# Sums of squares as one-column products, the second norm's factor moved to h, x1 made in chunks: one decoder layer on one core

## The reference

```python
xn = rmsnorm(x, norm_mix_pre)
x  = x + rmsnorm(W_o(sum_b sigmoid(g_b(xn)) * P_b(mixer_b(xn))), norm_mix_post)
hn = rmsnorm(x, norm_ffn_pre)
h  = hn @ w_up                        # 2 * 5632 columns: a gate half and a value half
hc = conv_b + sum(conv_w[i] * he[:, i:i + T] for i in range(3))   # he: two rows of history, then h
f  = (gelu(gate half of hc) * value half of hc) @ w_down
y  = x + rmsnorm(f, norm_ffn_post)

def rmsnorm(x, g):
    y = x * rsqrt(mean(x * x, -1) + 1e-6)
    return y * g
```

## Time and profile before

| | |
|---|---|
| median of 3 runs | 2102.45 us (2101.04 to 2105.14) |
| profiled execution | 2102.59 us, of this 2100.8 from the first to the last instruction (the span) |
| granted TensorE clock, mean of the span | 0.974 of full speed |
| instructions | 37670 |
| HBM | 374.87 MB read, 47.09 MB written |

### The profile page before, as it was taken

The page is one execution under the profiler, slowest core; times in us unless marked ns, Lnnn a source line. Parts: engine busy times, 40 slices in busy tenths (PEclk is TensorE's granted clock), DMA queues, the critical chain, the costliest instruction groups (busy, mean ns, idle before and its releaser), DMA issues.

```text
span 2100.8 us, 37670 instructions
## 1 busy us (share of the span) xinstructions
PE 2000.3 (95%) x15905; PEld 1918.4 (91%) x15905; DVE 1066.8 (51%) x1065; ACT 754.7 (36%) x641; POOL 94.5 (4%) x180
## 2 busy tenths in 40 slices
PE   7999996799999999999999699999999999999995
PEld 5999994599999999999999599999999999999994
DVE  4333334453444443445753656565665565565564
ACT  4333332334333433333333234333333333333332
POOL 0000002000000000000000101000000000000001
PEclk9999997799999999999999899999999999999998
DMA  6454522376666776766675234556566556566532
GB/s 240 162 173 163 185 80 80 125 253 213 220 223 226 253 254 209 227 198 233 245 233 170 80 121 161 163 177 216 200 211 222 195 204 223 203 212 205 204 119 61
DMA packets 187432, 396.15 MB, mean 189 GB/s; under 512 B 10745, under 2 KB 19985, under 8 KB 185786
## 3 DMA queue, kind: packets, MB, share of 16 engines
q1 hardware_dynamic: 182236, 359.38, 52.1%
q10 hardware_dynamic: 4567, 32.23, 3.8%
q0 software_dynamic: 528, 3.08, 0.5%
HBM read 374.87 MB, written 47.09 MB: 201 GB/s over the span
## 4 chain that ended last, share of the span: by engine, by line
PE 93%; DVE 5%; ACT 1%; issue 0%; DMA 0%; ACTq 0%; SPq 0%; DVEq 0%
PE ps L1556 27%; PE ps L1558 27%; PE ps L1557 27%; PE ps L1538 3%; PE ps L1544 1%; DVE m_T L1090 1%; PE ps L1812 1%; PE ps L1769 1%; PE ps L1775 1%; DVE w_lo L1073 1%; PE ps L1707 0%; PE ps L1800 0%; DVE stat L1083 0%; DMA x_nat<-in_x_prompt 0%; DVE vn L1178 0%
## 5 line engine op out<-in xcount | busy, mean ns | idle before, releaser
L1556 PE MATMUL ps<-xn_hi,w_hi 128*128 128x288 f32 x3104 | 922.0, 297 | 16.9 <-DVE xn_lo L1096 13.8
L1558 PE MATMUL ps<-xn_hi,w_lo 128*128 128x288 f32 x3104 | 917.5, 296 | 0.0
L1557 PE MATMUL ps<-xn_lo,w_hi 128*128 128x288 f32 x3104 | 916.0, 295 | 0.0
L1073 DVE TENSOR_TENSOR w_lo<-w_raw,w_hi 128x2048 fp32r<-128x2048 f32 (+1 forms) x272 | 614.4, 2259 | 570.7 <-ACT w_hi L727 570.7
L727 ACT ACTIVATE w_hi<-w_raw 128x2048 fp32r<-128x2048 f32 (+1 forms) x272 | 514.1, 1890 | 1018.8 <-PE ps L1558 1006.1
L1556 PEld LDWEIGHTS ps<-xn_hi,w_hi 128*128 128x128 f32 x3104 | 584.6, 188 | 25.6 <-DVE xn_lo L1096 15.4
L1557 PEld LDWEIGHTS ps<-xn_lo,w_hi 128*128 128x128 f32 x3104 | 584.6, 188 | 0.0
L1558 PEld LDWEIGHTS ps<-xn_hi,w_lo 128*128 128x128 f32 x3104 | 584.3, 188 | 0.0
L1556 PE MATMUL ps<-act_hi,w_hi 128*128 128x288 f32 x704 | 207.9, 295 | 2.8 <-DVE act_lo L1457 2.8
L1558 PE MATMUL ps<-act_hi,w_lo 128*128 128x288 f32 x704 | 208.5, 296 | 0.0
L1557 PE MATMUL ps<-act_lo,w_hi 128*128 128x288 f32 x704 | 207.9, 295 | 0.0
(11 more groups left out here) (266 smaller groups left out, 1529.6 us busy)
## 6 DMA issues: line engine op xcount, KB each, us to landing
w_raw<-in_w_in SPq DMA_DIRECT2D x104, 1024.0 KB, 6.6
w_raw<-in_w_up SPq DMA_DIRECT2D x88, 1024.0 KB, 5.0
w_raw<-in_w_down SPq DMA_DIRECT2D x44, 1024.0 KB, 5.2
k_half<-in_cache_k SPq DMA_DIRECT2D x64, 256.0 KB, 3.4
v_half<-in_cache_v SPq DMA_DIRECT2D x64, 256.0 KB, 3.3
w_raw<-in_w_o SPq DMA_DIRECT2D x16, 1024.0 KB, 5.2
out<-in_cache_win ACTq DMA_DIRECT2D x32, 512.0 KB, 4.4
w<-in_cache_win SPq DMA_DIRECT2D x40, 256.0 KB, 4.4
```

Of the source, the lines that this page charges most:

```text
L1073: e.tensor_tensor(w_lo[s][:, 0:k, 0:n], w_raw[slot][:, 0:k, 0:n], w_hi[s][:, 0:k, 0:n].bitcast(F32), ALU.subtract).then_inc(lo_ready, 1)
L1556: e.matmul(dst, w_hi[s][:, r, cols], x_hi[:, k0 + r, :], start=first and r == 0, stop=False)
L1557: e.matmul(dst, w_hi[s][:, r, cols], x_lo[:, k0 + r, :], start=False, stop=False)
L1558: mm = e.matmul(dst, w_lo[s][:, r, cols], x_hi[:, k0 + r, :], start=False, stop=last and r == k - 1)
```

## The change

Four things change.

- **Sums of squares.** The squares are first added together on DVE (`add_squares`), and PE then multiplies 128 tokens of squares as the stationary matrix with one column of ones (`col_sums`), so that the sums lie with tokens on the partitions: 128x3. Variance, root and reciprocal run on these three columns. A diagonal matrix with the factor and one product with ones bring it back to every partition.
- **The second norm's factor** is no longer applied to x1. `xn_hi` and `xn_lo` hold x1 times the gain alone, and `h_out` multiplies h by the factor as it takes it out of PSUM. For that `h_out` moves from ACT to DVE.
- **x1 in chunks.** `residual` makes x1 in eight chunks of 1, 1, 2, 2, 2, 2, 2 and 4 rows of 128; ACT and DVE make `xn_hi` and `xn_lo` chunk by chunk, and PE starts round 0 with the first.
- **Smaller moves.** W_o's groups get their gain at the copy from PSUM; the `hist_c` copy goes from DVE to ACT; `m_T` is cleared by POOL; at the end the squares stand ahead of the copies of `tail_rows`, and the factor is read from PSUM.

The core of the diff:

```diff
+        def x1_squares(q):
+            if q >= 2:
+                e.wait_ge(dve.sem, dve.at(("ffn_pre", "sum", q - 1)))
+            s = 1 if q == 1 else 0
+            e.activation(sq_x[s][:, :, :], x1[:, 4 * q:4 * q + 4, :], ACT.Square)\
+                .then_inc(act.sem, act.step(("ffn_pre", "sq", q)))
...
-        root("mix_post")
+        out_squares(3)
+        hi(ffn_unit(0, 1))
+        col_root("mix_post")
+        e.wait_ge(pe.sem, pe.at("histc"))
+        e.activation(view(hist_c, P, 0, [[1, 1408]]), view(ps, P, 0, [[1, 1408]]), ACT.Copy)\
+            .then_inc(act.sem, act.step("hist_c"))
+        high_chunks(0, 8)
+        hi(ffn_unit(0, 2))
+        high_chunks(8, 12)
+        hi(ffn_unit(0, 3))
+        high_chunks(12, 16)
         for q in range(4):
...
+            x1_squares(q)
...
-            h_out(i, 0, u0 + 4)
             hi(ffn_unit(i, 6))
...
-            h_out(i, 1, u0 + 8)
             e.wait_ge(conv_step, i * 24 + 12)
...
+        residual(0, 1)
+        residual(1, 1)
+        low_chunks(0, 1)
+        residual(2, 2)
+        low_chunks(1, 4)
+        lo(ffn_unit(0, 1))
+        residual(4, 2)
+        residual(6, 2)
+        low_chunks(4, 8)
+        lo(ffn_unit(0, 2))
...
+        def h_out(i, s, done):
+
+            e.wait_ge(unit_done, done)
+            e.wait_ge(conv_step, i * 24)
+            e.wait_ge(tails_put, i * 6)
+            e.wait_ge(pool.sem, pool.at(("H0", 1)))
+            e.wait_ge(act.sem, act.at(("ffn_pre", "rstd")))
+            e.tensor_tensor(H[s][:, :, 2:HS], ps[:, 4 * s:4 * s + 4, 0:NP_TOK],
+                            view(stat, P, 2 * TOK, [[0, 4], [1, NP_TOK]]), ALU.mult).then_inc(h_copied, 1)
...
+            h_out(i, 0, u0 + 4)
             conv_pair(i, 0, 0)
-            lo(ffn_unit(i, 7))
+            if down:
+                lo(ffn_unit(i, 7))
             conv_pair(i, 0, 2)
...
                 lo(ffn_unit(i, 9))
                 y_add(i, 0, ffn_unit(i, 8))
                 lo(ffn_unit(i, 10))
+            h_out(i, 1, u0 + 8)
             conv_pair(i, 1, 0)
...
+        def col_sums(tag, bank, at, sq, first):
+            for c in range(4):
+                for m, t0 in enumerate((0, P, TOK - P)):
+                    mm = e.matmul(ps[:, bank, at + m:at + m + 1], sq[:, c, t0:t0 + P], ones[:, 0:1],
+                                  start=first and c + m == 0, stop=False, skip_group_check=True)
+            return mm
...
+                    if fixed and i == 0 and s == 1 and j == 0:
+                        e.wait_ge(dve.sem, dve.at(("ffn_pre", "sum", 3)))
+                        col_sums("ffn_pre", 2, 288, sq_x[1], True).then_inc(pe.sem, pe.step(("ffn_pre", "ss")))
```

More of the change, by code:

```diff
@@ L687, in _ @@
         e.wait_ge(landed["x_back"], 16)
[L688 to L694, removed]
+        e.wait_ge(dve.sem, dve.at(("x1", 12)))
+        for q in range(4):
+            e.memset(m_T[:, 4 * q:4 * q + 4, :], 0.0).then_inc(y_added, 1)
+        e.wait_ge(act.sem, act.at("hist_c"))
         for s in range(2):
@@ L964, in _ @@
                 g = n // 4 - 1
[L965 to L968, removed]
-        root("mix_post")
-        for q in range(4):
[L971 to L987, removed]
+                out_squares(g)
+                for c in range(4):
+                    k = NORM["mix_post"] + 4 * g + c
+                    e.activation(m_T[:, 4 * g + c, :], ps[:, 4 * (g % 2) + c, 0:TOK], ACT.Identity,
+                                 scale=gains[:, k:k + 1]).then_inc(m_copied, 1)
+        out_squares(3)
[9 more added lines that the diff above has]
+        high_chunks(12, 16)
+        for q in range(4):
+            x1_squares(q)
         def act_high(i):
@@ L1017, in ffn_round @@
             window_copy(i, 0)
-            if early:
+            if early and down:
                 hi(ffn_unit(i, 2))
@@ L1021, in ffn_round @@
                 act_high(i)
-            for j in range(3 if early else 2, 6):
+            for j in range((3 if down else 4) if early else 2, 6):
                 hi(ffn_unit(i, j))
@@ L1025, in ffn_round @@
                     window_copy(i, j // 2)
-            h_out(i, 0, u0 + 4)
             hi(ffn_unit(i, 6))
+            if not down:
+                col_root("ffn_pre")
             hi(ffn_unit(i, 7))
+            if not down:
+                e.wait_ge(pe.sem, pe.at(("ffn_pre", "rstd")))
+                e.activation(view(stat, P, 2 * TOK, [[144, 2], [1, 144]]), view(ps, P, 288, [[512, 2], [1, 144]]), ACT.Copy)\
+                    .then_inc(act.sem, act.step(("ffn_pre", "rstd")))
             window_copy(i, 3)
@@ L1049, in _ @@
         hi(ffn_unit(11, 3))
+        e.wait_ge(tails_put, 66)
+        for q in range(4):
+            squares("ffn_post", m_T, sq_f, q, [(y_added, 4 + 4 * 10 + q + 1)])
         e.wait_ge(lo_ready, 272)
@@ L1055, in _ @@
             .then_inc(act.sem, act.step("tail_rows"))
-        for q in range(4):
-            squares("ffn_post", m_T, sq_f, q, [(y_added, 4 + 4 * 10 + q + 1)])
-        root("ffn_post")
+        col_root("ffn_post")
         for m in range(3):
@@ L1411, in _ @@
[L1411 to L1420, removed]
@@ L1421, in _, with add_squares, col_variance @@
-        variance("ffn_pre", 3, D_MODEL, ("ffn_pre", "ss", 3))
-        rstd("ffn_pre")
-        norm("ffn_pre", xw_b, x1, lambda q: None)
+        def add_squares(tag, sq, into, what, ready):
+            for q in ready:
+                e.wait_ge(act.sem, act.at((tag, "sq", q)))
+            e.tensor_tensor(into, sq, into, ALU.add).then_inc(dve.sem, dve.step((tag, "sum", what)))
+        def col_variance(tag, bank, at):
+            e.wait_ge(pe.sem, pe.at((tag, "ss")))
+            e.tensor_scalar(col[:, 0:3], ps[:, bank, at:at + 3], 1.0 / D_MODEL, EPS, ALU.mult, ALU.add)\
+                .then_inc(dve.sem, dve.step((tag, "var")))
@@ new lines, in low_chunks @@
+        def low_chunks(c0, c1):
+            for c in range(c0, c1):
+                g = NORM["ffn_pre"] + c
+                e.wait_ge(act.sem, act.at(("ffn_pre", "hi", c)))
+                e.scalar_tensor_tensor(out=xn_lo[:, c, :], in0=x1[:, c, :], scalar=gains[:, g:g + 1],
+                                       in1=xn_hi[:, c, :].bitcast(F32), op0=ALU.mult, op1=ALU.subtract)\
+                    .then_inc(dve.sem, dve.step(("ffn_pre", "lo", c)))
+        for j in range(2, 17):
+            lo(unit_no(U_GATE, 8, 0, j))
+            if j == 11:
+                add_squares("mix_post", sq_b[:, 0], sq_b[:, 1], 1, (0, 1))
+                e.wait_ge(dve.sem, dve.at(("mix_post", "sum", 1)))
+            if j == 15:
+                add_squares("mix_post", sq_b[:, 1], sq_b[:, 2], 2, (2,))
@@ L1474, in ffn_round @@
                 lo(ffn_unit(i, 1))
-            if fixed:
+            if fixed and down:
                 lo(ffn_unit(i, 2))
@@ L1482, in ffn_round @@
                 act_low(i)
-            for j in range(3, 7):
+            u0 = ffn_unit(i, 0)[0]
+            for j in range(3 if down else 4, 7):
                 lo(ffn_unit(i, j))
+            if not down:
+                col_variance("ffn_pre", 2, 288)
+                col_rstd("ffn_pre")
+                lo(ffn_unit(i, 7))
+            h_out(i, 0, u0 + 4)
             conv_pair(i, 0, 0)
-            lo(ffn_unit(i, 7))
+            if down:
+                lo(ffn_unit(i, 7))
             conv_pair(i, 0, 2)
@@ L1546, in sums, with unit @@
             mm.then_inc(pe.sem, pe.step((tag, "ss", q)))
-        def unit(no, x_hi, x_lo, k0, side, first, last, k=SEG, n=4):
+        def col_sums(tag, bank, at, sq, first):
+            for c in range(4):
+                for m, t0 in enumerate((0, P, TOK - P)):
+                    mm = e.matmul(ps[:, bank, at + m:at + m + 1], sq[:, c, t0:t0 + P], ones[:, 0:1],
+                                  start=first and c + m == 0, stop=False, skip_group_check=True)
+            return mm
+        def unit(no, x_hi, x_lo, k0, side, first, last, k=SEG, n=4, fresh=False):
             u, _, _, s = no
@@ L1948, in _ @@
                     unit(unit_no(U_GATE, 8, i, 4 * g + j), M_hi, M_lo, 4 * j, g, j == 0, j == 3)
-        e.wait_ge(m_copied, 3)
-        for q in range(4):
-            sums("mix_post", sq_b, q, 3)
+        e.wait_ge(m_copied, 12)
         e.wait_ge(landed["crow"], 16 * 8)
```

127 lines of the change are left out of this document (98 added, 29 removed).

## The result

The change is slower: 2169.26 us (median of 4 runs, 2165.68 to 2170.57) against 2102.91, a ratio of 1.0313 with a 95% interval of 1.0295 to 1.0332. The profiled execution took 2170.57, its span is 2168.8, the mean granted clock 0.957.

What follows compares the result with a forecast made beforehand. PE, busy 95%, was taken to bound the kernel, so any wait inside a round adds in full. 2102.6 + 74.7 (ten rounds) - 10 - 8 (the two ends) gave 2159 us, range 2138 to 2172.

Steps and rivals of the forecast that it cites:

- The mechanism: Rounds 1 to 10: unit 9 waits 5.83 us for h_out(i,1) on DVE, behind y_add(i,0) and w_lo of unit 10.
- Case B: Ahead of unit 9: h_out(i,1) is through before unit 8 ends, so no wait; 2084.6 us, chance 0.05.
- The clock's term: Behind unit 9's wait, 17 products at the 1.2 GHz level lose 1.64 us per round, bounds 0 and 1.64.
- Case A: Rounds 1 to 10: the stalls come without a clock loss; 2143 us, chance 0.08.
- The sum: Whole kernel: 2102.6 plus 74.7 for the rounds, less 10 and 8 for the two ends, 2159.3 us.
- part 2: From the last W_o unit to the first FFN products: 27.6 us earlier, mostly given back; 10 gained, 6 to 16.
- part 3: End of the kernel: sums, scaling and adds finish sooner, 8 us gained, bounds 5 to 10.
- main case: Whole kernel: waits ahead of unit 9 less gains at both ends, 2159 us, ends 2135 and 2171, chance 0.83.
- Case C: Feed-forward rounds: POOL's copies of the tails hold DVE's convolution, 11 us more, 2171; chance 0.04.

Runs made afterwards that it cites:

- The early version: The change with h_out(i,1) on DVE moved between w_lo of unit 8 and w_lo of unit 9, ahead of y_add(i,0): 2089.89 us.
- The third experiment: The change plus 14 extra fp32 products on PE, results thrown away, between y_add(i,0) and unit 9 of each of ten rounds: 2148.04 us.
- the second experiment: The change with h_out(i,1) moved between y_add(i,0) and w_lo of unit 10: 2128.32 us.
- the last experiment: The early version, with ACT copying the last norm's factor from PSUM to SBUF for the 16 scalings: 2092.03 us.

## Why the prediction was right, point by point

**The mechanism** held to the row: the place (unit 9 of rounds 1 to 10), the releaser (`H` by DVE) and the order behind unit 8's end. A wait of 5.83 was forecast and an idle time of 5.73 came; `h_out` took the 1.42 that it had been given (1573.38 to 1574.80). Case B ended the other way for the reason given: neither `y_add(i,0)` nor w_lo of unit 10 can start before unit 8 ends. The early version is what case B described, and at 2089.89 it lies near the 2084.6 worked out for it.

**The clock's term** was right in kind and too small: 1.64 per round were taken and called the upper bound too, "since a longer wait costs no second restart". A round takes 84.40 us ((2080.76 - 1321.20) / 9, the first and the last of the ten waits), 8.1 over 76.3. The third experiment, in which the clock did not fall, puts 6.0 of this down to the wait and 2.1 to the clock. The 2.1 is a mean: behind the ten waits between 11 and 25 products came at 0.24 us, a loss of 1.4 to 2.8. Behind 1574.92 and behind 1827.68 it is, over 4 us:

```profile
1575.00:1579.00 4.00, 4.00 (x21) 0.65 0.72 255
1828.00:1832.00 4.00, 4.00 (x18) 0.50 0.68 249
```

So the 1.64 of the earlier trace rows was no ceiling. It was no floor either: behind the 2.85 of the second experiment nothing was lost in four rounds of ten, and in the third experiment the wait of the earlier trace rows itself, again 2.81, was followed by a clock of 1.00 (2085 to 2089). Nor is a wait just above the 1.55 of the earlier trace rows safe: after one of 1.96, at 998.37 in the kernel before, the clock was 0.50 from 1000 to 1002. A single row was taken for a fixed price; the price varies from wait to wait, and what decides it stays open.

Ten rounds came to 81.2 for 74.7, which is 6.5 of the 10 us by which 2159 was too low, about 1.6 of them wait and 4.9 clock. Case A, no clock loss, would have been 2143; the experiment with extra products brought it about and came to 2148.

**The sum.** In the profiled execution 11.3 us lie between 2159.3 and 2170.6: 6.5 from the rounds, 2.6 from part 2, 2.5 from the spread ahead of W_o's end, less 0.3 from part 3. The upper end of the main case, 2171, had been built from a dearer `h_out` and smaller gains. A dearer `h_out` did not come; that the clock's excess fitted into the same room is luck.

**Part 2** gave 7.4 where 10 were taken and 6 to 16 allowed. The first product came 13.5 us after W_o's end (1173.75 to 1187.23), not 11.75. Of these 1.7 us the one-column products are 1.5: 7.06 for 5.6. The waits ahead of units 2 to 4 were smaller than forecast (1.47, 1.90 and 4.06 for 1.8, 2.0 and 6.1), and there was none ahead of unit 1. The clock went the other way: two restarts, 3.2 us, were counted, but behind the start of units 3, 4 and 5 the products lost about 5.6 us at the 1.2 GHz level, after waits of 1.90 and 4.06 and, in unit 5, after the one-column products of the second norm. Two of these stretches:

```profile
1212.00:1216.00 4.00, 3.67 (x16) 0.57 0.20 79
1236.00:1240.00 4.00, 4.00 (x21) 0.57 0.25 50
```

That part 2 came out near its forecast is in part two errors that cancelled: 3.5 us less of waits, about 2.4 more of clock.

**Part 3** gave 8.3 for 8. The split between its steps was not foreseen: the one-column products took 8.45 for 5.6 to 6.6, and scaling from 2146.60 came 13.9 after the last `y_add` began, where it was 18.6 before, so 4.7 earlier and not 7. The scalings and adds made up for it. What scaling and adds themselves gave is 3.1 (from the first scaling's start to the last add's end 14.45 before, 11.32 now): the scalings were no longer held beside POOL's add, but DVE's own adds were, 2.18 for 1.36.

The rule that the prediction cited from the Trainium skill, "SBUF — State Buffer", section "SBUF: two separate sides" (a VectorE operation with two SBUF inputs and a GpSimd operation that reads SBUF exclude each other for a whole instruction), agrees with the trace of the last experiment: eight scalings take 5.88 with the factor in SBUF and 3.49 with it in PSUM.

**Case C** didn't come: the first tap beside POOL's copy took 0.86 for 0.78, and the second and third taps, which read two SBUF tensors, took 528 ns on average in both kernels. But the earlier trace rows had been read wrongly. The copy ran 1.14 there and ended as w_lo ended, and now it takes:

```profile
1574.96 0.19 POOL L705 COPY tails<-H 128x8 f32 x1 [24.51 <-DVE H L1507]
```

All 22 of these copies took 1.12 to 1.14 us before, and 0.19 to 0.36 now. So by these rows it was POOL that waited for DVE in the kernel before; the row said nothing of what POOL would do to DVE.

## What to carry to other kernels

In all rows shown here DVE took its operations in the order written, waiting at each until it could start. So an operation that frees a buffer must not stand behind one that needs the work which waits for that buffer. When a step moves to another engine, list what stands ahead of it there and what each of those waits for: engine shares (DVE was at 51%) say nothing about it, and here a shift by three places in the order is worth 81 us.

A wait of PE inside a dense stretch can cost more than its length, and not the same each time: nothing or 1.5 us more behind waits of 2.85, 1.4 to 2.8 more behind waits of 5.73. Take the price from several waits at least as long, or leave both ends open.

Where a small gain has to be seen under a larger spread, cut both spans at the same events and compare stretches; medians gave 3.5 us for an end that is worth 8.

## What the runs showed of the hardware that was not expected

The clock also fell while PE was busy without a pause. During the 48 records of one-column products behind W_o the granted clock went from 1.00 to 0.50, and the records came half as often:

```profile
1175.00:1177.00 2.00, 2.00 (x22) 1.00 0.67 260
1177.00:1179.00 2.00, 2.00 (x18) 0.86 0.00 0
1179.00:1181.00 2.00, 2.00 (x11) 0.50 0.00 0
```

PE shows no idle time in these stretches; what it did ahead of the fall were these products. In the kernel before, the sums over 288 columns stand at this place, and from 1171 to 1179 the granted clock was 1.00. The fall is a part of why the one-column sums took 7.06 and 8.45 where the sums over 288 columns had taken 7.92 and 9.72. In the third experiment the 28 records over 144 columns were followed by a clock of 1.00. What in the products makes the difference was not tried.
